# Two attention layers and a mixer with experts in one kernel: layers unrolled, the p product at a layer's head, softmaxes and norms reordered

## The reference

```
h = x @ w_in            # split into a_q a_k a_v a_z | b_cq b_ckv b_kr b_z | c_q c_k c_v c_z
ya = moba_attention(a_q, a_k, a_v) * silu(a_z)      # 8 heads of 64, ALiBi, causal
cq, ckv = rmsnorm(b_cq), rmsnorm(b_ckv)             # the latents, 384 and 256 wide
yb = mla_attention(cq @ w_uq (+rope), ckv @ w_ukv, rope(b_kr)) * silu(b_z)
yc = rmsnorm(diff_attention(c_q, c_k, c_v)) * silu(c_z)
g = sigmoid(x @ w_merge + b_merge)                  # three parts of 1024
out = (ga*(ya @ w_a) + gb*(yb @ w_b) + gc*(yc @ w_c)) @ w_out
r = ALPHA*x + out
r = r + sigmoid(r @ w_pg) * (p_i @ w_p)             # p_i: 256 x 256, w_p: 256 x 1024
x = layernorm(r)
```

## Time and profile before

| what | value |
|---|---|
| median of 3 runs | 2311.03 us (2310.81 to 2312.49) |
| profiled execution, its own time | 2310.84 us |
| its span, first to last instruction | 2309.3 us |
| mean granted TensorE clock | 0.981 |
| PE, PEld | 2211.1 us (96%), 1950.4 us (84%) |
| DVE, ACT, POOL | 1367.9 (59%), 1204.1 (52%), 451.3 us (20%) |
| chain that ended last | PE 76%, issue 12%, POOL 7%, DVE 2%, ACT 2%, DMA 1% |
| first block, two layers | from 0 to about 779 us |

### The profile page before, as it was taken

One profiled execution on the slowest core, in us unless ns is written; L12 is line 12 of the kernel. 1 busy time (PEld: TensorE's weight loads), 2 busy tenths in 40 slices (PEclk: granted clock), 3 DMA queues, 4 the chain that ended last, 5 costly groups with the idle time before them and its releaser, 6 DMA issues.

```text
span 2309.3 us, 33386 instructions
## 1 busy us (share of the span) xinstructions
PE 2211.1 (96%) x12737; PEld 1950.4 (84%) x12738; DVE 1367.9 (59%) x1379; ACT 1204.1 (52%) x1295; POOL 451.3 (20%) x223
## 2 busy tenths in 40 slices
PE   7999998999999798999998999999999999999997
PEld 6879997988998797999897888888888888888885
DVE  1354213236411485100384798898989898989895
ACT  3445312445430453222353576777767676767773
POOL 6615521634550300454400000000000000000000
PEclk8999999999999999999999999999999999999998
DMA  6334455424353352555443799999989898989992
GB/s 202 111 97 159 147 167 165 128 81 157 128 200 129 98 160 69 174 177 182 130 146 110 271 377 355 344 363 342 376 327 372 327 377 327 371 326 378 354 356 91
DMA packets 306371, 528.32 MB, mean 229 GB/s; under 512 B 11360, under 2 KB 152192, under 8 KB 306272
## 3 DMA queue, kind: packets, MB, share of 16 engines
q1 hardware_dynamic: 306080, 526.44, 64.6%
q0 software_dynamic: 192, 0.48, 0.1%
HBM read 525.84 MB, written 1.05 MB: 228 GB/s over the span
## 4 chain that ended last, share of the span: by engine, by line
PE 76%; issue 12%; POOL 7%; DVE 2%; ACT 2%; DMA 1%; POOLq 0%; DVEq 0%; SPq 0%; ACTq 0%
PE bank L614 74%; POOL weights_low L2454 7%; PE bank L1212 1%; DVE gc L1805 1%; ACT L1314 1%; DMA ring<-in_w_out_dram 0%; DMA ring<-in_w_in_dram 0%; ACT rs L1314 0%; DVE expert_weights_low L1797 0%; DVE cat L1805 0%; DVE h L1805 0%; ACT xT L1314 0%; ACT expert_weights_high L1317 0%; PE bank L1305 0%; DVE rstd L1977 0%
## 5 line engine op out<-in xcount | busy, mean ns | idle before, releaser
L1797 DVE TENSOR_TENSOR expert_weights_low<-ring_experts,expert_weights_high 128x2048 fp32r<-128x2048 f32 x336 | 765.4, 2290 | 93.6 <-ACT expert_weights_high L1317 93.0
L1317 ACT ACTIVATE expert_weights_high<-ring_experts 128x2048 fp32r<-128x2048 f32 x336 | 645.5, 1922 | 177.4 <-PE bank L614 177.4
L2454 POOL TENSOR_TENSOR weights_low<-ring,weights_high 128x1024 fp32r<-128x1024 f32 x176 | 427.5, 2454 | 666.0 <-ACT weights_high L1317 666.0
L1317 ACT ACTIVATE weights_high<-ring 128x1024 fp32r<-128x1024 f32 x216 | 220.3, 1053 | 368.1 <-PE bank L614 113.1
L614 PE MATMUL bank<-expert_weights_high,gathered_high 128*128 128x512 f32 x896 | 356.6, 398 | 1.4 <-DVE gathered_low L1797 1.4
L614 PE MATMUL bank<-expert_weights_high,gathered_low 128*128 128x512 f32 x896 | 349.3, 390 | 0.0
L614 PE MATMUL bank<-x_high,weights_high 128*128 128x256 f32 x896 | 259.6, 290 | 16.6 <-DVE x_high L1872 14.3
L614 PE MATMUL bank<-x_high,weights_low 128*128 128x256 f32 x896 | 252.9, 283 | 0.0
L614 PE MATMUL bank<-x_low,weights_high 128*128 128x256 f32 x896 | 249.8, 284 | 0.0
L614 PE MATMUL bank<-expert_weights_low,gathered_high 128*128 128x512 f32 x896 | 239.7, 389 | 0.0
L614 PE MATMUL bank<-h_high,weights_high 128*128 128x256 f32 x704 | 203.6, 291 | 12.5 <-ACT h_high L1317 12.5
(11 more groups left out here) (257 smaller groups left out, 3126.0 us busy)
## 6 DMA issues: line engine op xcount, KB each, us to landing
ring_experts<-in_moe_w_gate_dram SPq DMA_DIRECT2D x112, 1024.0 KB, 5.3
ring_experts<-in_moe_w_up_dram SPq DMA_DIRECT2D x112, 1024.0 KB, 5.3
ring_experts<-in_moe_w_down_dram SPq DMA_DIRECT2D x112, 1024.0 KB, 5.2
ring<-in_w_in_dram SPq DMA_DIRECT2D x62, 1024.0 KB, 5.2
ring<-in_w_merge_dram SPq DMA_DIRECT2D x24, 1024.0 KB, 5.3
ring<-in_w_out_dram SPq DMA_DIRECT2D x16, 1024.0 KB, 5.1
ring<-in_ffn_w_gate_dram SPq DMA_DIRECT2D x11, 1024.0 KB, 5.2
ring<-in_ffn_w_up_dram SPq DMA_DIRECT2D x11, 1024.0 KB, 7.4
```

The lines of the kernel that those rows point to most:

```text
L1317: return nc.scalar.activation(dst, src, ACT.Copy, scale=scale)
L1797: return nc.vector.tensor_tensor(dst, x, z, op)
L2454: nc.gpsimd.tensor_tensor(half_of(wlo[:, q_slot, :], t), half_of(ring[:, slot, :], t), half_of(whi[:, q_slot, :], t).bitcast(F32), ALU.sub ...
```

## The change

The loops over the layers are written out on all engines. In the ring's order p and w_ple become the first two units of a layer, aq0 the third; az0's weights move ahead of w_uq. In TensorE's order pt and pl0 to pl3 come first, ahead of aq0; dk0 comes ahead of B 0; V 1 and A 2 come between mc0 and mc1; mc1, mc2, ms, B 2 and az0 follow, then V 2 and A 3; az1 alone stays between B 3 and V 3. The product with w_ple gets a tile of its own (pleT), cn shares cq's place, peT that of sc. At the end of layer 0 ScalarE still splits the next layer's aq0 behind pg2's tanh, but aq1 only at the head of layer 1; it drains pt and pl0 between the steps of the layer norm. The three inverse roots of a layer become Ln and Exp on ScalarE, straight from PSUM, with no step on DVE. At the start SyncE loads only the 128 columns of the identity, then x (into y), p, w_ple, aq0's weights, and then the rest of the constants; the turned x goes to banks 4 to 7, and ScalarE copies it before it splits aq0. The core of the diff:

```diff
 ORDER1 = [
+    ("pt", "a"), ("pl0", "a"), ("pl1", "a"), ("pl2", "a"), ("pl3", "a"),
     ("aq0", "a"), ("aq1", "a"), ("ak0", "v"), ("ak1", "v"), ("av0", "a"), ("av1", "a"), ("A", 0),
-    ("dq0", "a"), ("dq1", "a"), ("B", 0), ("dk0", "v"), ("dk1", "v"), ("V", 0), ("A", 1),
-    ("dv0", "a"), ("dv1", "a"), ("B", 1), ("mc0", "a"), ("mc1", "a"), ("V", 1), ("A", 2),
-    ("mc2", "a"), ("pt", "a"), ("pl0", "a"), ("pl1", "a"), ("ms", "v"), ("B", 2), ("pl2", "a"),
-    ("pl3", "a"), ("V", 2), ("A", 3), ("uq0", "a"), ("uq1", "a"), ("uq2", "a"), ("uq3", "a"),
+    ("dq0", "a"), ("dq1", "a"), ("dk0", "v"), ("B", 0), ("dk1", "v"), ("V", 0), ("A", 1),
+    ("dv0", "a"), ("dv1", "a"), ("B", 1), ("mc0", "a"), ("V", 1), ("A", 2),
+    ("mc1", "a"), ("mc2", "a"), ("ms", "a"), ("B", 2), ("az0", "v"), ("V", 2), ("A", 3),
+    ("uq0", "a"), ("uq1", "a"), ("uq2", "a"), ("uq3", "a"),
...
-    ("az0", "v"), ("az1", "v"), ("V", 3), ("A", 4), ("bz0", "v"), ("bz1", "v"), ("B", 4),
-    ("cz0", "v"), ("cz1", "v"), ("V", 4), ("A", 5), ("dn0", "v"), ("dn1", "v"),
+    ("az1", "v"), ("V", 3), ("A", 4), ("bz0", "v"), ("bz1", "v"), ("B", 4),
+    ("cz0", "v"), ("cz1", "v"), ("V", 4), ("A", 5), ("dn0", "a"), ("dn1", "a"),
...
-    ("lm", "v"), ("lv", "v")]
+    ("lm", "v"), ("lv", "a")]
 UNITS1 = (
-    [("w_in", c, 256, 8) for c in range(0, 1536, 256)]
+    [("p", 0, 256, 2), ("w_ple", 0, 1024, 2)]
+    + [("w_in", c, 256, 8) for c in range(0, 1536, 256)]
     + [("w_in", c, 256, 8) for c in range(3232, 3232 + 1536, 256)]
-    + [("w_in", 2048, 256, 8), ("w_in", 2304, 256, 8), ("w_in", 2560, 160, 8)]
-    + [("p", 0, 256, 2), ("w_ple", 0, 1024, 2)]
+    + [("w_in", 2048, 256, 8), ("w_in", 2304, 256, 8), ("w_in", 2560, 160, 8), ("w_in", 1536, 256, 8)]
...
-            sp.dma_start(cst[:, :], a["cst"]).then_inc(cst_in, 16)
-            sp.dma_start(sq[:, :, :].rearrange("p (t a) s -> p t (a s)", t=TT),
+            sp.dma_start(cst[:, 0:P], a["cst"][:, 0:P]).then_inc(ident_in, 16)
+            sp.dma_start(y[:, 0:DT, :].rearrange("p (t a) s -> p t (a s)", t=TT),
                          a["x"][0].rearrange("(t p) d -> p t d", p=P)).then_inc(x_in, 16)
-            with sp.Fori(0, LAYERS) as layer:
+            for layer in range(LAYERS):
...
+                    if layer == 0 and u == RING - 1:
+                        sp.dma_start(cst[:, P:], a["cst"][:, P:]).then_inc(cst_in, 16)
...
+            def inv_std(dst, src, e, log, at_log):
+
+                fn(dst, src, ACT.Ln, bias=eps[:, e:e + 1]).then_inc(log, 1)
+                act.wait_ge(log, at_log)
+                return fn(dst, dst, ACT.Exp, scale=-0.5)
...
             for b in range(4):
                 act.wait_ge(x0_full, b + 1)
-                copy(xT[:, 2 * b:2 * b + 2, :], views(b)).then_inc(x_ready.h, 2)
+                copy(xT[:, 2 * b:2 * b + 2, :], views(4 + b)).then_inc(x_ready.h, 2)
+            drain(0, "pt", peT)
+            split1(0, 0)
+            for j in range(4):
+                drain_ple(0, j)
...
+                after("mc0")
+                latent(0)
                 take_y(1)
                 exps(2)
+                latent(1)
...
                     fn(tmp[:, j % 2, :], bank[b][:, :], ACT.Tanh, scale=0.5).then_inc(dr_a.h, 1)
-                    if j >= 2:
+                    if j == 2 or (j == 3 and layer == LAYERS - 1):
                         after(f"mg{8 + j}")
...
-                G1.wait_drained(act, layer, "lv")
-                fn(rstd[:, 0, :], rstd[:, 0, :], ACT.Sqrt).then_inc(ln_std.h, 1)
+                b = G1.wait_full(act, layer, "lv")
+                inv_std(rstd[:, 0, :], views(b)[:, 0, :], 0, dr_a.h, drained_at(layer, "lv")).then_inc(ln_std.h, 1)
+                ahead = layer + 1 < LAYERS
+                if ahead:
+                    drain(layer + 1, "pt", peT)
                 for t in range(DT):
...
+                    if ahead and t == 3:
+                        drain_ple(layer + 1, 0)
+                if ahead:
+                    for j in range(1, 4):
+                        drain_ple(layer + 1, j)
...
-                b = G1.wait_full(dve, layer, "lv")
-                ts(rstd[:, 0, :], views(b)[:, 0, :], 1e-5, None, ALU.add).then_inc(dr_v.h, 1)
                 dve.wait_ge(ln_std.h, ln_std.at(layer, 1))
-                link(nc.vector.reciprocal(rstd[:, 0, :], rstd[:, 0, :]))
```

More of the change, by code:

```diff
@@ L897, in layer_body @@
                 assert unit[0] == len(UNITS1)
-            with pe.Fori(0, LAYERS) as layer:
+            for layer in range(LAYERS):
                 layer_body(layer)
@@ L1336, in free @@
                     if t == 0 and before[1] != "v":
-                        act.wait_ge(used.h, used.at(layer, q - 1))
+                        act.wait_ge(used.h, layer * len(SPLIT1) + q - 1)
                     else:
-                        G1.wait_full(act, layer, before)
-                split(u % RING, landed[0].at(layer, 16 * (u // RING + 1)), q % 2, free)
-            for q in range(2):
-                split(SPLIT_AT[q], 16, q, None)
+                        G1.wait_full(act, turn, before)
@@ L1504, in layer_body @@
                         x_ready.h, 1)
-            with act.Fori(0, LAYERS) as layer:
+                    if ahead and t == 3:
[3 more added lines that the diff above has]
+                        drain_ple(layer + 1, j)
+            for layer in range(LAYERS):
                 layer_body(layer)
@@ L1815, in layer_body @@
             def layer_body(layer):
-                turn[0] = layer
                 def drain(name, dst):
@@ L1980, in layer_body @@
                         ALU.mult, ALU.mult).then_inc(normed.h, 1)
-            dve.wait_ge(x0_full, 4)
-            with dve.Fori(0, LAYERS) as layer:
+            for layer in range(LAYERS):
                 layer_body(layer)
-            assert link_at[0] == vlink.per, f"vector steps of a layer: {link_at[0]}"
-            turn[0], link_at[0] = LAYERS, 0
             def low_part(k, n):
```

178 lines of the change are left out of this document (93 added, 85 removed).

## The result

The changed kernel takes 2318.48 us (median of 10, 2315.29 to 2321.81), the kernel before 2310.92 beside it: ratio 1.0033, 95% interval 1.0024 to 1.0043. It is slower, by 7.6 us; the forecast was 2304.8 and its range ended at 2313. The profiled execution took 2316.71 us with a span of 2314.5, against 2310.84 and 2309.3: 5.2 us of span to explain. Another 0.7 us lies outside the span: 2.2 us in every execution of the changed kernel and its variants (2.1 to 2.3), 1.5 in those of the kernel before (1.5 to 1.6), and 1.8 to 1.9 where that one is only written out.

A forecast was written before the change was run, and what follows sets the result against it. TensorE was taken as nearly always busy within a layer, so only its holes count. Gains of 4.1 (head), 14.2 (two layers) and 0.4 (layer 1's end) less 12.5 (boundary) gave 6.2 us: 2304.8 us, range 2297 to 2313.

The forecast's parts named there:

- VectorE's two steps (1.4 us): Layer boundary: DVE's two steps queued behind pg3's delayed tanh, ahead of lm's last quarter, taken at 1.4 us.
- dk0's 1.2: Each layer: dk0 ahead of the first turn of probabilities shrinks the hole there; gain 1.2 us, bounds 0.6 and 2.2.
- Head: Start of layer 0: earlier x makes room for the p product, aq1 starts sooner; gain 4.1 us, bounds 2.9 and 4.9.
- Middle: Inside each layer: p product leaves for 9.1 us, less four answers; gain 7.1 per layer, 14.2 for two.
- (2) A2: Each layer: y reaches A2 late because ScalarE splits az0 before copying y; loss 1.5 us, bounds 0.3 and 2.
- (3) ms: Each layer: ms comes right behind mc2, whose squares nothing covers now; loss 1.2 us.
- (4) dn: Each layer: third inverse root by Ln and Exp with two table loads delays mg2; loss 0.7 us, bounds 0 and 1.
- Boundary: Between layers: aq0's split waits for its slot ahead of pg3's tanh, breaking lm, and p product follows lv; loss 12.5 us.
- B: Layer boundary: slot comes free earlier, pg3's tanh isn't held up, boundary costs only 2.0; 2294.4 us, chance 0.08.
- C: Inverse roots: one table load serves Ln and Exp, at dn, boundary and last norm; 2299.4 us, chance 0.04.
- D: Middle of layers: third softmax's neighbours leave large holes, another 3 us late per layer; 2311 us, chance 0.06.
- A: Head and boundary: clock stays low during p product, costing about 6 and 9.4 us; 2320 us, chance 0.08.

The follow-up runs named there:

- the best one: Changed kernel with layer 1's aq0 split behind the last norm's root, y copied before az0's split, third inverse root by square root and reciprocal: 2298.05 us, ratio 0.9933.

## Why the prediction was wrong

Faster by 6.2 us was forecast, and it came out slower. Four terms of the sum failed: the second block, taken at 0, costs 2 us (5.3 in the profiled execution); "VectorE's two steps (1.4 us)" at the boundary took 4.2; the middle of a layer gained 4.6 and 4.7 us where 7.1 was forecast, mainly because dk0's 1.2 did not come; and "1.5 around it", the time outside the span, is 2.2.

**Head: right in the mechanism, low for the profiled pair.** 4.1 forecast with bounds of 2.9 and 4.9, 5.56 in the profiled pair. The term that was off is the clock: it was taken to come back at 14.7, and here the p product ran at full clock from its start (7.14 us as one row). That is the forecast's bound "at once", and nine of thirteen profiles have it; in the other four the clock came back between 15.3 and 15.8, much as forecast. Over all profiles A0 is at 53.4 in the mean of thirteen with the new head and at 56.9 in that of four with the old, so the gain is 3.5: inside the bounds. The pair gave more because the kernel before had its latest A0 of four in it (58.40).

**Middle: 4.6 and 4.7 instead of 7.1.** The 9.1 for the p product holds. (1) dk0: "gain 1.2" is 0 in the profiled pair and 0.4 in the mean of all profiles; the hole shrank by 0.5 as reckoned, but "some of the time at the low clock behind it" had the wrong sign in the pair (0.71 for 0.80). (2) A2: nearly as forecast. It waits 0.67 us, and the broken turn takes 2.87 us until mc1 starts (109.35 to 112.22) where the unbroken one took 1.61 (120.57 to 122.18): 1.3 of the 1.5. The landing behind it varies, and in two later profiles it made the wait 2.2 and 2.8, with mc1 at a lower clock behind it; a bound of 2 does not hold those. (3) ms: 1.2, as forecast. (4) dn: 0.8 at mg2's start and 0.4 inside it, 1.2 instead of 0.7, even above the bound of 1: the second half of the weights was not followed. And one hole was not on the list: cz0 waits for its low part (its start comes 0.6 us later than back to back). Its split stands behind the softmax's exponentials and bz0's tanh in both kernels, but the exponentials now come 0.9 us later against TensorE: with az1 alone ahead of V3, VectorE is still at work on mv and az1's gate (one step of it 1.84 us instead of 1.23, beside GpSimd) when the scores of A4 are there, and begins on them 1.2 us behind bz0's start (174.63, 173.42), where it was 0.3 (185.70, 185.42). 7.1 less 1.2 (dk0), 0.5 (dn) and 0.6 (cz0), and 0.2 back from A2, gives 5.0; the remaining 0.4 lies where az0 was moved away from: az0, az1, V3 and A4 take 15.70 us by their starts instead of 15.34, which the forecast had at nothing.

**Boundary: the mechanism right, 15.25 instead of 12.5.** ScalarE's 12 us of waiting, the broken lm, the low clock and the p product behind lv came as described. The term that failed is "VectorE's two steps (1.4 us)": they took 4.2 beside GpSimd, and the run that kept them apart gives back 3.4. From lv's end to A0 the change adds 1.85 (43.98 against 42.13), where 2.0 was forecast. The 0.7 us is right for the kernel before, where the two steps start at 386.16 and 386.88 and GpSimd only at 387.15; the forecast did not ask what the same landing starts on GpSimd.

**Last norm: right** (0.46 against 0.4). **Second block: 0 was wrong** by 2 us in most executions and by 5.3 in the profiled one. "Runs the same code" is no reason for the same time when the clock's stretches fall elsewhere. Thirteen profiles with the long mean have 1531.2 to 1532.0 us (nine) or 1534.9 to 1538.3 (four); five with the short one 1529.3 to 1529.8. The 3 to 7 us more in those four have two sources. In the first profile 3.0 are the product with w_out from 1249.97 on (0.66 granted, 1.00 before). In the other three the 4.4 to 6.2 us lie in the last 25 us of the span, and they begin as a late start: the last mean of the kernel starts 6.1 to 6.7 us behind the start of its squares on ScalarE, where it is 0.7 to 1.2 in all other profiles, and the profile names nothing that TensorE waits for. Why is open.

Sum: the forecast's span is 2303.1 (2309.3 less 6.2), the measured one 2314.5. Of the 11.4 between them 5.3 lie in the second block, 4.9 in the two middles and 2.75 at the boundary; 1.5 came back at the head. The median was forecast at 2304.8 and is 2318.48: 11.4 of the 13.7 us are these, 0.7 lies outside the span, and the profiled execution was 1.8 faster than the median of its ten. Of the rivals B is refuted (lm was broken), C as well (two loads each), and D (no hole at its places). A is refuted as it was priced: the p product ran at full clock at both places in the profiled execution. In part it does happen: in four of the thirteen profiles with the early x the first part of the product at the head ran at 1.2 GHz (9.0 to 9.2 us for 7.1), and in four of the later runs the one at the boundary took 8.6 to 8.8. That is 1.5 to 2 us a place, while A wanted 6 and 9.4. So the time ended near its 2320 for other reasons.

## What to carry to other kernels

Where a transfer's landing starts work on two engines at once, look at what the third engine is doing then: GpSimd's operation over SBUF made VectorE's two-input steps 2 to 4 times as long, at two places of these kernels, each time in front of TensorE. A split or cast that waits for a slot of a ring belongs behind everything in its engine's order that is ready earlier; that one move was worth 9.6 of the 17.7 us between the changed kernel (2315.75) and the best one (2298.05). And a shorter kernel can come out longer by some 2 us per place because the stretches at 1.2 GHz fall on other instructions: look at several profiles before a difference of that size is given a cause.

## What the hardware showed

- A pause 2.1 us longer in front of the mixer's mean went with 2.1 us less behind the mean's start (1529.5 us against 1531.6; the first profile's 1534.9 has 3.0 more at another place); one 0.9 us longer in the kernel before made it 2.2 longer (1532.0 against 1529.8).
- The mean's length is nearly the same in the two profiles of each kernel (6.39 and 6.33; 5.27 and 5.26), though the starts differ by 2.2 us. Why they agree so well is open, and two profiles of each are few.
- A p product of 32 matmuls took 7.14 us at full clock and 8.6 to 9.2 where its first part ran at 1.2 GHz, its matmuls 0.43 us apart instead of 0.22; the same kernel had either in different executions.
- VectorE's steps of 0.69 us took 1.51 and 2.71 beside GpSimd's subtraction, and two that take 1.83 together took 4.0. Both times a delayed step ended 0.55 us behind the GpSimd instruction beside it.
- Each switch between Ln and Exp is a load of 1.28 us, and the next instruction starts within 0.02 us of its end.
